# Transposing instead of multiplying: gate rows, and the weighted values of a neighbourhood attention, in a two-part transformer kernel on one core

## The reference, cut to what matters

```
x = x + 0.5 * gate * swiglu(modulate(x, g, shift, scale), w_in, w_out)
x = x + gt * y          # after a mixer
```

```
y_a = neighbourhood_attention(qa, ka, va, kax, vax, rpb)     # 8 heads of 64
y_b = mlstm_readout(h_b, ob, head_g)                          # 4 heads of 128
y   = concatenate([y_a, y_b], axis=-1) @ w_out

# neighbourhood attention, for one head and one row of the grid (4 rows of 64):
s = concatenate([q k_window * scale + bias, q k_context * scale])
p = softmax(s)
o = p_loc @ v_window + p_ctx @ v_context

# read-out of the mLSTM
y = rms_norm(h, head_g) * sigmoid(o)
```

## Time and profile before

| | |
|---|---|
| median of 3 runs | 1600.84 us (1600.77 to 1601.09) |
| the profiled execution's own time | 1601.29 us |
| its span, first to last instruction | 1599.5 us |
| granted clock of TensorE, mean | 0.999 |
| TensorE, VectorE, ScalarE busy | 99%, 73%, 49% |
| gates at (us from the span's start) | 137.9, 284.7, 435.0 (two), 869.6, 1010.6, 1198.2, 1378.4, 1530.6 |
| neighbourhood attention, from its first scores to its last sums | 808.8 to 869.5 us |

### The profile page before, as it was taken

How to read it: one execution, slowest core, us unless ns; L and a number is a source line. 1 busy time by engine, 2 the same in 40 slices (tenths; PEclk the granted TensorE clock), 3 DMA queues, 4 the chain that set the end, 5 groups by cost and what they waited for, 6 DMA issues and landing times.

```text
span 1599.5 us, 21020 instructions
## 1 busy us (share of the span) xinstructions
PE 1578.1 (99%) x8130; PEld 1316.2 (82%) x8130; DVE 1173.0 (73%) x1917; ACT 776.7 (49%) x1242; POOL 70.4 (4%) x112
## 2 busy tenths in 40 slices
PE   7999999999999999999999999999999999999998
PEld 5788778888888888887777888888888888888887
DVE  7889899769876665468655888868877667666654
ACT  5767667432312222354555555545555463455542
POOL 2000000100000000120010100000000100010000
PEclk9999999999999999999999999999999999999999
DMA  9977675336656664251121787757787575455550
GB/s 378 369 293 274 234 248 210 106 145 224 223 202 233 213 229 163 86 179 67 66 100 66 275 301 293 300 226 258 258 286 258 214 304 190 166 202 191 186 182 29
DMA packets 93046, 336.99 MB, mean 211 GB/s; under 512 B 10625, under 2 KB 11265, under 8 KB 92690
## 3 DMA queue, kind: packets, MB, share of 16 engines
q1 hardware_dynamic: 90706, 327.58, 56.3%
q0 software_dynamic: 2240, 8.06, 1.5%
HBM read 334.56 MB, written 1.05 MB: 210 GB/s over the span
## 4 chain that ended last, share of the span: by engine, by line
PE 55%; DVE 2%; issue 1%; ACT 0%; POOL 0%; POOLq 0%; DVEq 0%; ACTq 0%
PE bank L292 53%; PE bank L295 2%; DVE sb_tm L301 0%; DVE sb_XN L309 0%; DVE sb_XN L301 0%; DVE sb_X L301 0%; DVE sb_arena L312 0%; DVE sb_arena L319 0%; ACT sb_XN L298 0%; DVE sb_sg L316 0%; DVE sb_XC L301 0%; DVE sb_w7r L301 0%; DVE sb_w5r L301 0%; POOL sb_rstd L301 0%; DVE sb_arena L309 0%
## 5 line engine op out<-in xcount | busy, mean ns | idle before, releaser
L292 PE MATMUL bank<-sb_hT,sb_hi 128*128 128x512 f32 (+1 forms) x1856 | 575.0, 380 | 0.0
L298 ACT ACTIVATE sb_hi<-sb_w 128x1024 fp32r<-128x1024 f32 x428 | 431.4, 1052 | 287.5 <-DMA sb_w<-in_w 243.2
L292 PEld LDWEIGHTS bank<-sb_hT,sb_hi 128*128 128x128 f32 x1856 | 332.3, 189 | 58.4 <-issue 0.2
L292 PE MATMUL bank<-sb_hi,sb_hT 128*128 128x512 f32 x1152 | 370.0, 396 | 2.5 <-ACT sb_hT L298 1.3
L292 PEld LDWEIGHTS bank<-sb_hi,sb_hT 128*128 128x128 f32 x1152 | 215.8, 188 | 53.0 <-issue 5.3
L312 DVE CUSTOM_DVE_ANT_0 sb_w<-sb_w,sb_cb 128x1024 f32<-128x1024 f32 x144 | 174.9, 1219 | 0.0
L301 DVE TENSOR_TENSOR sb_sg<-bank,sb_sg 128x512 f32<-128x512 f32 (+1 forms) x90 | 58.9, 660 | 102.1 <-ACT sb_sg L298 80.0
L298 ACT ACTIVATE sb_sg<-bank 128x512 f32<-128x512 f32 (+1 forms) x98 | 54.8, 572 | 117.3 <-PE bank L292 117.0
L298 ACT ACTIVATE sb_arena<-bank 128x512 f32<-128x512 f32 (+1 forms) x106 | 56.3, 558 | 54.2 <-PE bank L292 31.8
L301 DVE TENSOR_TENSOR sb_tm<-bank,sb_rows 128x512 f32<-128x512 f32 (+1 forms) x41 | 28.1, 684 | 71.4 <-PE bank L292 68.6
L298 ACT ACTIVATE sb_XN<-sb_X 128x512 f32<-128x512 f32 x33 | 20.7, 629 | 100.5 <-DVE sb_X L301 92.4
(11 more groups left out here) (483 smaller groups left out, 3245.4 us busy)
## 6 DMA issues: line engine op xcount, KB each, us to landing
sb_w<-in_w SPq DMA_DIRECT2D x428, 512.0 KB, 4.3
sb_w<-in_mw SPq DMA_DIRECT2D x192, 512.0 KB, 4.6
sb_rows<-in_na_rpb POOLq DMA_DIRECT2D x16, 96.0 KB, 2.9
sb_X<-in_x SPq DMA_DIRECT2D x1, 1024.0 KB, 5.0
sb_cb<-in_cvec POOLq DMA_DIRECT2D x2, 512.0 KB, 9.4
sb_XC<-in_ctx POOLq DMA_DIRECT2D x1, 1024.0 KB, 13.2
sb_arena<-in_sg_ln_g POOLq DMA_DIRECT2D x1, 1024.0 KB, 5.8
sb_arena<-in_sg_ln_b POOLq DMA_DIRECT2D x1, 1024.0 KB, 10.2
```

What stands on the lines that cost most here:

```text
L292: return self.e.matmul(out, a, b, start=start, stop=stop)
L298: return self.e.activation(out, a, f, **kw)
```

## The change

Three things are changed.

- `pe_gate` transposes the broadcast column in place of multiplying it by the identity.
- In the neighbourhood attention the operands of the weighted sum are exchanged: the values of a head (128x64) are stationary and the turned probabilities of both halves of the tokens move (256 columns). Two heads write the lower and the upper 64 partitions of bank 7. So y comes out transposed, in the layout that the output projection needs, and the eight transposes of the last item fall away. A group is two heads and all their steps; there are four, at v = 3, 5, 7 and 9, in place of two steps at each v from 2 to 9. `NP` becomes larger, two buffers of a whole head each, over the whole of `XC`, and its refilling waits for the group before. The shares (reciprocals of the sums) have to be spread along the rows: ScalarE repeats each over 64 columns into SG[3] (v = 4 and 8), TensorE transposes that (v = 5 and 9; the first time into a bank of the ring `AB`), ScalarE copies the bank into y, and VectorE multiplies bank 7 by it. The split for the projection then reads y, in two parts, at u = 29 and 31.
- In the mLSTM's end, phase 5 moves from u = 27 to u = 25 and multiplies by the gain alone; the sigmoid is multiplied in afterwards, at `o`, into y. On ScalarE, the exponent of step 13 moves from item 6 behind the split of phase 6.

```diff
@@ pe_gate
-                    m = e.mm(b.ap[:, c4 * 128:(c4 + 1) * 128], mods[:, TG[target], c:c + 1].to_broadcast([128, 128]),
-                             ident, True, True)
+                    m = e.tr(b.ap[:, c4 * 128:(c4 + 1) * 128], mods[:, TG[target], c:c + 1].to_broadcast([128, 128]), ident)
@@ the table
-        NP = [xcf[:, i * 512:(i + 1) * 512] for i in range(2)]
+        NP = [xcf[:, i * 1024:(i + 1) * 1024].rearrange("p (j x c) -> p j x c", j=2, x=4) for i in range(2)]
-        MX[27][1:1] = [("o", 0), ("ml", (None, 5))]
+        MX[25].append(("ml", (None, 5)))
+        MX[27].insert(1, ("o", 0))
         MX[27].append(("ml", (None, 6)))
-        MX[31] += [("gate", 0), ("y", 0)]
+        MX.setdefault(29, []).append(("y", 0))
+        MX[31] += [("gate", 0), ("y", 1)]
@@ act_mlstm, phase 6
                     act_split(e, ("y", "mx", 1), myT[1], 4, [done(PVS, "ml", 3, 1)])
+                    act_neighbour_exp(e, 13)
@@ dve_mlstm, phase 5
+                    e.wait_ge(*done(DE, "half_gain"))
                     for j in range(2):
-                        e.wait_ge(*done(DE, "sig", j))
                         for h4 in range(4):
                             m = e.stt(y[:, j, c], y[:, j, c], hr[:, j * 4 + h4:j * 4 + h4 + 1],
-                                      sig[:, j, h4 * 128:(h4 + 1) * 128], ALU.mult, ALU.mult)
+                                      hg[:, h4 * 128:(h4 + 1) * 128], ALU.mult, ALU.mult)
@@ dve_projected_mixer, o
-                    e.stt(sig[:, j, :], sig[:, j, :], 1.0, hg, ALU.add, ALU.mult).then_inc(DE.sem, DE.put("sig", j))
+                    e.wait_ge(*done(DE, "mg", j))
+                    e.stt(y[:, j, 512:1024], sig[:, j, :], 1.0, y[:, j, 512:1024], ALU.add, ALU.mult).then_inc(
+                        DE.sem, DE.put("my", *(() if j else (j,))))
@@ pe_neighbours
-            if v >= 2:
-                pe_neighbour_sums(e, 2 * v - 4)
-                pe_neighbour_sums(e, 2 * v - 3)
+            if v in (3, 5, 7, 9):
+                pe_neighbour_sums(e, v // 2 - 1)
             if 1 <= v <= 8:
                 pe_neighbour_turn(e, 2 * v - 1)
+            if v in (5, 9):
+                pe_neighbour_spread(e, v // 4 - 1)
@@ pe_neighbour_sums
+            b, o = bank[7], p % 2 * 256
+            for n in range(4 * p, 4 * p + 4):
+                e.wait_ge(*done(AE, "nPT", n))
             for x in range(4):
-                m = e.mm(b.ap[:, o:o + 64], NP[n % 2][:, x * 128:(x + 1) * 128], nv[:, x, h * 64:h * 64 + 64], x == 0, x == 3)
+                for h in (2 * p, 2 * p + 1):
+                    po = 64 * (h % 2)
+                    m = e.mm(b.ap[po:po + 64, o:o + 256], nv[:, x, h * 64:h * 64 + 64], NP[h % 2][:, :, x, :], x == 0, x == 3)
@@ new on TensorE
+        def pe_neighbour_spread(e, g):
+            b = BANK["nR", g] = HB3.take() if g else bank[(AB.i + 1) % 4]
+            ...
+            e.wait_ge(*done(AE, "na_recip", g))
+            for i in range(2):
+                for j in range(2):
+                    c = i * 256 + j * 128
+                    m = e.tr(b.ap[:, c:c + 128], SG[3][:, j * 256 + i * 128:j * 256 + i * 128 + 128], ident)
@@ act_neighbours
+                if v in (5, 9) and x:
+                    act_neighbour_spread(e, v // 4 - 1)
-                if v < 8:
+                if v < 8 and (v, x) != (6, 1):
                     act_neighbour_exp(e, 2 * v + x)
+            if v in (4, 8):
+                act_neighbour_repeat(e, v // 4 - 1)
@@ act_neighbour_turn
-            if n >= 2:
-                e.wait_ge(*done(PVS, "na", n - 2))
+            if h >= 2:
+                e.wait_ge(*done(PVS, "na", h // 2 - 1))
@@ dve_neighbours
+            if v in (4, 8):
+                e.wait_ge(*done(EX, "na", 2 * v - 1))
+                e.recip(na_shares(v // 4 - 1), na_shares(v // 4 - 1)).then_inc(DE.sem, DE.put("na_recip", v // 4 - 1))
+            if v in (6, 9):
+                dve_neighbour_sums(e, v // 9)
@@ dve_neighbour_sums
+            e.wait_ge(*done(AE, "nR", g))
+            e.wait_ge(*done(PVS, "na", g * 2 + 1))
+            e.tt(y[:, g, 0:512], bank[7].ap[:, :], y[:, g, 0:512], ALU.mult).then_inc(DE.sem, DE.put("O", "na", g))
```

More of the change, by code:

```diff
@@ L2270, in pe_mixer @@
                         pe_gate(e, "m01gt", HB3)
-                    elif what == "y":
-                        pe_transposes(e, ("y", "mx", 0), y, 0, 4, [done(DE, "O", "na", 1)], HB3,
-                                      lambda c2: ((DE, "y", "mx", 0, c2),))
             for j in range(2):
@@ L2501, in dve_mlstm @@
                             m = e.stt(y[:, j, c], y[:, j, c], hr[:, j * 4 + h4:j * 4 + h4 + 1],
-                                      sig[:, j, h4 * 128:(h4 + 1) * 128], ALU.mult, ALU.mult)
-                            m.then_inc(DE.sem, DE.put("my", *(() if j * 4 + h4 == 7 else (j, h4))))
+                                      hg[:, h4 * 128:(h4 + 1) * 128], ALU.mult, ALU.mult)
+                            m.then_inc(DE.sem, DE.put("mg", j, *(() if h4 == 3 else (h4,))))
                 elif ph == 6:
@@ L2549, in pe_neighbour_turn, with pe_neighbour_sums @@
             b.till = ((AE, "nPT", n),)
[L2551 to L2555, removed]
+        def pe_neighbour_sums(e, p):
+            b, o = bank[7], p % 2 * 256
+            if p % 2 == 0:
                 for f in b.free():
                     e.wait_ge(*f)
-            e.wait_ge(*done(AE, "nPT", n))
+            for n in range(4 * p, 4 * p + 4):
+                e.wait_ge(*done(AE, "nPT", n))
             for x in range(4):
@@ L2561, in pe_neighbour_sums @@
             for x in range(4):
-                m = e.mm(b.ap[:, o:o + 64], NP[n % 2][:, x * 128:(x + 1) * 128], nv[:, x, h * 64:h * 64 + 64], x == 0, x == 3)
-            m.then_inc(PVS.sem, PVS.put("na", n))
-            b.till = ((DE, "O", "na", n // 8),)
+                for h in (2 * p, 2 * p + 1):
+                    po = 64 * (h % 2)
+                    m = e.mm(b.ap[po:po + 64, o:o + 256], nv[:, x, h * 64:h * 64 + 64], NP[h % 2][:, :, x, :], x == 0, x == 3)
+            m.then_inc(PVS.sem, PVS.put("na", p))
+            b.till = ((DE, "O", "na", p // 2),)
+        def pe_neighbour_spread(e, g):
+            b = BANK["nR", g] = HB3.take() if g else bank[(AB.i + 1) % 4]
+            for f in b.free():
+                e.wait_ge(*f)
+            e.wait_ge(*done(AE, "na_recip", g))
[3 more added lines that the diff above has]
+                    m = e.tr(b.ap[:, c:c + 128], SG[3][:, j * 256 + i * 128:j * 256 + i * 128 + 128], ident)
+            m.then_inc(TRP.sem, TRP.put("nR", g))
+            b.till = ((AE, "nR", g),)
         def act_neighbours(e, v):
@@ L2623, in dve_neighbour_sums, with neighbour_rows @@
         def dve_neighbour_sums(e, g):
[L2624 to L2631, removed]
+            e.wait_ge(*done(AE, "nR", g))
+            e.wait_ge(*done(PVS, "na", g * 2 + 1))
+            e.tt(y[:, g, 0:512], bank[7].ap[:, :], y[:, g, 0:512], ALU.mult).then_inc(DE.sem, DE.put("O", "na", g))
+        def neighbour_rows(g):
+            return y[:, g, 0:512].rearrange("p (a b) -> p a b", a=2)
         def act_mixer(e):
@@ L2669, in act_mixer @@
                     elif what == "y":
-                        act_split(e, ("y", "mx", 0), myT[0], 4, [done(SCO, "na", 15)])
+                        e.wait_ge(*done(SCO, "na", 15))
+                        e.wait_ge(*done(DE, "O", "na", i))
+                        e.act(myT[0][0][:, 2 * i:2 * i + 2, :], neighbour_rows(i), ACT.Copy).then_inc(
+                            AE.sem, AE.put("y", "mx", 0, i))
                 if u == 0:
@@ L2676, in act_mixer @@
                             square(e, "cx1", XC, j, nh, SQ, [done(RES, "ctx", 6, j, nh), *rows_turned("m01")])
-            act_edge(e, "m02", W_MX + 32, ("mx",), (0, 1), [done(TRP, "y", "mx", 0, 1)], hT_free("m02"))
+            act_edge(e, "m02", W_MX + 32, ("mx",), (0, 1), [done(DE, "y", "mx", 0, 1)], hT_free("m02"))
         def act_projected_mixer(e, kind):
@@ L2775, in dve_mixer @@
                         dve_projected_mixer(e, "o")
-                        dve_neighbour_sums(e, 0)
                     elif what == "pf":
@@ L2784, in dve_mixer @@
                     elif what == "y":
-                        e.wait_ge(*done(DE, "O", "na", 1))
-                        dve_split(e, ("y", "mx", 0), myT[0], 4)
+                        c = slice(2 * i, 2 * i + 2)
+                        e.wait_ge(*done(AE, "y", "mx", 0, i))
+                        e.tt(myT[0][1][:, c, :], neighbour_rows(i), myT[0][0][:, c, :].bitcast(F32), ALU.subtract).then_inc(
+                            DE.sem, DE.put("y", "mx", 0, i))
                 if u == 1:
```

20 lines of the change are left out of this document (17 added, 3 removed).

## The result

The changed kernel takes 1588.84 us (median of 4 runs, 1588.80 to 1589.21) against 1600.80 us for the kernel before (4 runs beside it, 1600.66 to 1601.09). The ratio is 0.9925, with a 95% interval of 0.9912 to 0.9937: 12.0 us faster. The forecast was 1589.5 us and faster.

The account below looks back on a forecast made before the run. TensorE, busy 1578.1 of 1599.5 us, was taken to bound the kernel. Gates outside the mixer -5.5 and mixer -5.8 sum to -11.3 us: 1600.84 to 1589.5 us, range 1585.8 to 1594.0 us.

Parts of the forecast that it names:

- Gates: Nine gates, each 0.92 us shorter by transposes; two early ones worth 0, six outside the mixer 5.5 us, m01 in mixer.
- the rival: First gates of both layers: each keeps its 0.92 us, giving 1587.7 us; chance 0.08.
- Group of sums: Mixer's weighted values: two heads overlap, 16 records of 256 columns take 1.87 us a group.
- the added 0.13 for its neighbours: 0.13 us added to each 1.87 us group for two neighbours that start later, making 2.0 us.
- The bank wait of na 2 and na 4: Mixer items 2 and 4: second turn waits for VectorE's masked minimum; 0.5 us returns plus 0.06 restarting, -1.17 each.
- na 5 and na 6: Mixer items 5 and 6 with the mLSTM half: ScalarE is late next, split at 848.7 against 849.53, -0.83 us.
- The rival by which the mixer is bound by its chain: Mixer's exponents and copies: no gain at items 5/6, 0.5 us more per item with scores; 1592.3 us, chance 0.14.
- na 9, gate, y: Mixer's item 9 to projection's second half: 4.7 us to first need, some 0.4 us waiting against 0.6; -1.6 us.
- The rival by the Trainium skill (TensorE: Matmul & The Clock Gate, Part 4): TensorE's gate transposes: full clock does not engage, gates give nothing; slower by the clock, 1605 us, chance 0.03.

Follow-up runs that it names:

- the run with another bank: Changed kernel with the second turn of items na 2 and na 4 put in a free bank of the other ring (AB): 1588.13 us, ratio 0.9918.
- The last kernel above (bias behind): Changed kernel with second turns in the other ring's bank, first spread later, and na 1's two VectorE bias instructions behind its masked minima: 1586.70 us.
- the one with one head after the other: Changed kernel with the two loops of a group of sums exchanged, four context blocks of one head and then the other's: 1592.41 us, ratio 0.9946.
- the gates alone: Kernel before with only the nine gates done by transposes: 1594.94 us, ratio 0.9961.
- the early gates alone: Kernel before with transposes only at the first-stage gates of both layers, products at the other seven: 1600.95 us, ratio 0.9999.

## Why the prediction was right, step by step

- **Gates.** 0.92 us each, and which are kept: right. The two early ones gave nothing (0.2 us in the median of their own run, inside its interval; the 1.84 us of the rival lie outside it), the other seven 6.2 us of 6.4.
- **Group of sums.** 1.87 us and the overlap: right; the added 0.13 for its neighbours was right too (+0.30 and +0.27 for the items that have a group in place of a pair). That what a group has beyond 8 x 0.216 us, 0.14 us, is the cost of changing the mode is not shown: the first product behind eight ordinary transposes takes 0.32 us to the next start (858.66 to 858.98) where 0.23 is usual.
- **The bank wait of na 2 and na 4.** Right in place, releaser and size: TensorE's turn at 821.29 us, 0.34 us on VectorE, 0.56 us with the restart; the run with another bank takes exactly this away.
- **na 5 and na 6.** The chain was the right one and link by link as told: sums, turn 8's copy, exponent 10, turn 9, spread, exponent 11, turn 10, exponent 12, turn 11, split. Measured from the scores of na 5, turn 8's copy stands at 3.54 us (predicted 3.49) and the split at 8.06 (predicted 8.29). The term that was off is an exponent with its read: I took 0.78 us to the next start from the earlier trace rows, but there the copy behind it had to wait for TensorE's turn, which ends only at 844.15 us; ScalarE's timeline after shows 0.70, three times 0.08:

```profile
840.09 0.60 ACT L298 ACTIVATE sb_XC<-bank 128x512 f32<-128x512 f32 x1 [2.25 <-PE bank L292]
840.59 0.71 ACT L298 ACTIVATE sb_arena<-sb_arena,sb_nast 128x512 f32<-128x512 f32 x1
...
841.29 0.59 ACT L298 ACTIVATE sb_XC<-bank 128x512 f32<-128x512 f32 x1
...
844.61 1.11 ACT L298 ACTIVATE sb_myT1h<-bank 128x512 fp32r<-128x512 f32 x2
```

Of the two moves in the mLSTM part, the exponent is worth 0.7 us. The multiplications could as well have stayed in unit 27. The rival by which the mixer is bound by its chain wanted no gain here and 0.5 us more in every item with scores; the table has neither.
- **na 9, gate, y.** -1.61 against -1.6. The first need of the second half comes 4.81 us behind the sums (predicted 4.7); it stands 0.40 us behind the start before it, where 0.23 is usual, and its low part 0.63 where 0.46 is usual: 0.34 us of waiting for the 0.4 in the sum. The close match of the whole is in part luck: my terms give 5.0 + 0.2 before and 3.3 + 0.4 after, which is 1.5 us less and not the 1.6 that I wrote. TensorE after, from the sums (the earlier trace rows before):

```profile
861.57 1.95 PE L292 MATMUL bank<-sb_XC,sb_arena 128*64 128x256 f32 x16
863.45 0.66 PE L295 MATMUL bank<-sb_cst,sb_sg 128*128 128x128 f32 x4
863.94 1.04 PE L295 MATMUL bank<-sb_cst,sb_mods 128*128 128x128 f32 x8
864.74 0.48 PE L292 MATMUL bank<-sb_hi,sb_myT0h 128*128 128x512 f32 x1
...
866.38 0.47 PE L292 MATMUL bank<-sb_hi,sb_myT0h 128*128 128x512 f32 x1
```

- **The clock and the transposes.** The rival by the Trainium skill (TensorE: Matmul & The Clock Gate, Part 4), by which transposes do not engage the full clock, does not hold here. Where the clock already was at its full level, f32 transposes kept it at 1.00 for 10.3 us. For a low one I had overlooked the start of every kernel here, where TensorE stands for over 3 us and then transposes XN 16 times. The last kernel above (bias behind), and then the one with one head after the other:

```profile
9.37 3.85 PE L295 MATMUL bank<-sb_cst,sb_XN 128*128 128x128 f32 x16 [3.39 <-ACT sb_XN L298]
12.97 1.17 PE L292 MATMUL bank<-sb_hi,sb_hT 128*128 128x512 f32 x4
13.99 0.39 PE L292 MATMUL bank<-sb_w2r,sb_hT 128*128 128x512 f32 x1
```

```profile
13.07 2.06 PE L292 MATMUL bank<-sb_hi,sb_hT 128*128 128x512 f32 x4
14.92 0.80 PE L292 MATMUL bank<-sb_w2r,sb_hT 128*128 128x512 f32 x2
```

These 16 transposes take 3.60 us, from the third on 0.213 us from start to start where those above took 0.108: the lower level, 1.2 GHz. The profile prints a granted clock of 1.00 here too, but the first record of the clock in this trace is at 12.95 us, so the pace has to be read, and the forty full slices of the earlier trace rows say nothing of the first 13 us. From there on the level is full: four products take 1.02 us, where the other kernel, whose first record of the clock is at 15.27 us, needs 1.85. When the clock rose in the first of these two kernels, TensorE had done nothing but transposes since it stood. In the other thirteen traces it rose behind the start of one to five products. The kernel before and the changed one differ little in it (13.41 and 13.16 us).
- **Not in the sum: the end.** 0.57 us of the 12.1 came after TensorE's last start. See below.

The forecast was 0.7 us too high. The end (0.57) and the exponents (0.24) make 0.8; the other lines of the table are off by 0.07 at most and nearly cancel.

## What to carry to other kernels

A saving on the busiest engine is worth its size only where no other chain is just in time behind it, so go through the places one by one: here two of nine equal cuts gave nothing, and the trace of before said which. Take an instruction's price from a place where the next one did not wait. When an instruction list gets shorter, ask which wait it had covered: the sums that left na 2 and na 4 uncovered a wait for a bank, which one line gave back.

## What was not expected of the hardware

**The last store and the code.** From TensorE's last start (1592.45 and 1580.92 us) to the end are 7.02 us before and 6.45 after, while VectorE's and ScalarE's rows between are the same to 0.02 us. The DMA of the last 9.5 us, before and then after (queue and kind: packets, MB, share; then the stores of the output, KB each and median us from issue to landing):

```profile
q14 instruction: 1, 0.01, 0.4%
...
out_x<-sb_XN SPq DMA_DIRECT2D x4, 256.0 KB, 2.3
```

```profile
q1 hardware_dynamic: 576, 1.05, 29.3%
...
out_x<-sb_XN SPq DMA_DIRECT2D x4, 256.0 KB, 2.0
```

Before, one packet of code moves beside the output: it starts 2.67 us before the end, while the last two stores run. The kernel before, the gates alone and the early gates alone have this packet, stores of 2.3 us and ends of 6.9 to 7.2 us; the ten other kernels here and the changed one have none, stores of 2.0 us and ends of 6.4. The packet takes 0.65, 0.74 and 0.58 us in the three (the packed traces' own records), and their ends are 0.57, 0.75 and 0.49 us longer than 6.45. That the packet delays the store fits all fourteen traces. But the three that have it are also the three that keep the mixer of before, and none moved the packet alone, so it is not shown.

**Overlap reaches past neighbours.** Products into the two halves of a bank's partitions need not alternate: with eight of one head and then eight of the other, the second head started four records early, and half of the gain was kept.

**The start.** The first scores of na 0 stand at 807.18, at 807.05 or 807.06, or between 806.73 and 806.87 us in the profiled runs of ten kernels that are the same up to there. The moment at which the clock rises (12.95 to 15.43 us) does not go with it: 12.95 us has 806.73, 13.16 has 807.06, and 15.27 has 806.87. A difference of 0.3 us between two single runs is therefore not told apart here.
